# Time mixing in diagonal blocks of 64 tokens, in opposite quadrants of the array

## The reference

```python
def step(state, inp):
    r_t, w_t, k_t, v_t, kk_t, a_t = inp
    sa = jnp.einsum('bhvk,bhk->bhv', state, -kk_t)
    state = (state * w_t[:, :, None, :] + sa[..., None] * (kk_t * a_t)[:, :, None, :]
             + v_t[..., None] * k_t[:, :, None, :])
    return state, jnp.einsum('bhvk,bhk->bhv', state, r_t)
...
_, ys = lax.scan(step, s0, xs)
```

## Time and profile before

| What | Value |
|---|---|
| Time, median of 3 runs | 2509.83 us (2509.53 to 2512.68) |
| Profiled execution | 2512.97 us, its span 2511.3 us |
| PE busy | 2338.5 us (93%), 15533 instructions |
| PE weight loads busy | 1588.8 us (63%) |
| DVE busy | 777.9 us (31%) |
| ACT busy | 365.3 us (15%) |
| Chain that ended last | PE 86%, DVE 11%, ACT 1%, issue 1% |
| Mean granted TensorE clock | 0.937 |

### The profile page before, as it was taken

How to read it: one execution, slowest core, us unless ns; L and a number is a source line. 1 busy time by engine, 2 the same in 40 slices (tenths; PEclk the granted TensorE clock), 3 DMA queues, 4 the chain that set the end, 5 groups by cost and what they waited for, 6 DMA issues and landing times.

```text
span 2511.3 us, 35417 instructions
## 1 busy us (share of the span) xinstructions
PE 2338.5 (93%) x15533; PEld 1588.8 (63%) x15533; DVE 777.9 (31%) x1511; ACT 365.3 (15%) x746; POOL 0.2 (0%) x4
## 2 busy tenths in 40 slices
PE   8887899999987799999999999988889999989998
PEld 5686577766677576655545546455657776656775
DVE  2546346512545420011010010013734652641001
ACT  2411200011421210000000101013220001221001
POOL 0000000000000000000000000000000000000000
PEclk9976899999977799999999999998889999979999
DMA  5210398504210189989989989613229840308410
GB/s 216 84 51 1 119 427 328 193 1 164 94 51 1 71 336 405 394 347 392 410 350 418 425 334 361 262 70 147 107 108 419 323 190 26 109 35 354 154 54 17
DMA packets 55167, 524.08 MB, mean 209 GB/s; under 512 B 6368, under 2 KB 6880, under 8 KB 16864
## 3 DMA queue, kind: packets, MB, share of 16 engines
q1 hardware_dynamic: 45792, 471.43, 46.5%
q10 hardware_dynamic: 9216, 50.34, 5.3%
HBM read 520.69 MB, written 1.05 MB: 208 GB/s over the span
## 4 chain that ended last, share of the span: by engine, by line
PE 86%; DVE 11%; ACT 1%; issue 1%; DMA 0%; DVEq 0%; SPq 0%; ACTq 0%
PE ps L89 86%; DVE ring L89 6%; DVE stat L89 1%; DVE transposed L89 1%; DVE natural L89 1%; DVE gates L89 1%; ACT ring L89 0%; DVE residual L89 0%; DMA ring<-in_moe 0%; ACT z L89 0%; ACT L89 0%; ACT stat L89 0%; DMA constants<-in_const 0%; ACT transposed L89 0%; DVE z L89 0%
## 5 line engine op out<-in xcount | busy, mean ns | idle before, releaser
L89 PE MATMUL ps<-ring 128*32 128x256 f32 (+9 forms) x7636 | 587.5, 345 | 14.9 <-DVE ring L89 5.3
L89 PEld LDWEIGHTS ps<-ring 128*32 128x32 f32 (+4 forms) x7636 | 409.3, 129 | 188.3 <-issue 63.5
L89 PE MATMUL ps<-transposed,ring 128*128 128x256 f32 x2112 | 466.4, 379 | 5.2 <-issue 2.3
L89 PE MATMUL ps<-ring,transposed 128*128 128x384 f32 (+4 forms) x1408 | 470.6, 493 | 0.1
L89 PE MATMUL ps<-ring,z 128*32 128x512 f32 (+2 forms) x1936 | 459.1, 594 | 0.6 <-issue 0.3
L89 PEld LDWEIGHTS ps<-transposed,ring 128*128 128x128 f32 x2112 | 401.0, 190 | 85.8 <-issue 31.2
L89 PEld LDWEIGHTS ps<-ring,transposed 128*128 128x128 f32 x1408 | 266.6, 194 | 188.6 <-issue 65.4
L89 DVE TENSOR_TENSOR z<-z,ps 128x256 f32<-128x256 f32 (+3 forms) x146 | 58.7, 402 | 885.4 <-ACT z L89 855.3
L89 PEld LDWEIGHTS ps<-ring,z 128*32 128x32 f32 (+2 forms) x1936 | 169.4, 139 | 213.1 <-issue 203.7
L89 ACT ACTIVATE z<-ps 128x256 f32<-128x256 f32 (+2 forms) x151 | 56.2, 372 | 943.5 <-PE ps L89 933.6
L89 ACT COPY z<-ps 128x384 f32<-128x384 f32 (+6 forms) x166 | 67.9, 409 | 699.0 <-PE ps L89 697.4
(11 more groups left out here) (129 smaller groups left out, 1147.3 us busy)
## 6 DMA issues: line engine op xcount, KB each, us to landing
ring<-in_moe SPq DMA_DIRECT2D x88, 2048.0 KB, 12.0
ring<-in_ffn SPq DMA_DIRECT2D x66, 1536.0 KB, 15.3
ring<-in_moe SPq DMA_DIRECT2D x88, 1024.0 KB, 10.4
ring<-in_w_in SPq DMA_DIRECT2D x26, 1536.0 KB, 6.8
z<-in_ada ACTq DMA_DIRECT2D x48, 768.0 KB, 6.9
ring<-in_w_out SPq DMA_DIRECT2D x12, 1536.0 KB, 6.3
natural<-in_ada ACTq DMA_DIRECT2D x16, 768.0 KB, 8.1
ring<-in_ple_gate SPq DMA_DIRECT2D x4, 1536.0 KB, 6.5
```

Source lines behind the costliest of these rows:

```text
L89: self.ins = None if self.book.counting else op(*args, **kw)
```

## The change

The parts of the time mixing that stay inside a chunk now compute only the blocks on the diagonal. A masked square is stored as 128 partitions by 64 columns: partitions 0 to 63 hold the block of the first chunk, 64 to 127 that of the second. The masks shrink alike, and `ident64` is a stacked pair of identities. Where one product of 128 by 128 stood, two of 64 by 64 stand, c = 0 from partitions 0 to 63 to PSUM partitions 0 to 63 and c = 1 from 64 to 127 to 64 to 127: opposite quadrants, in the same bank. The functions `rw_inv`, `rw_invT` and `chunk` name these pieces.

All squares of one tile's scores (i) fit into two banks, so both tiles' scores are issued together before the last projection tile and masked by two DVE instructions per tile. The inverse and its transpose lie side by side in `gates`, and an update fills one bank per half, so that one subtraction does both. The first turn is a product with `ident64` instead of a transpose. The copies of the kp factor go ahead, behind the last level. Both layers have the change.

```diff
-    strict, incl = (s < t) & same, (s <= t) & same
-    one["mask4"] = np.concatenate([strict, incl, strict, incl], 1)
+    sc, tc = s % 64, np.arange(64)[None, :]
+    one["ident64"] = (sc == tc)
+    one["mask4"] = np.concatenate([sc < tc, sc <= tc, sc < tc, sc <= tc], 1)
...
-    rw_prod = Carve(work, rw_shared)(8, 4, P)
+
+    rw_prod = Carve(work, rw_shared)(8, 4, HD)
     xc, gc = Carve(xt_flat), Carve(gates_flat)
-    rw_inv, rw_invT, rw_lev, rw_cx = xc(8, P), xc(8, P), gc(8, P), gc(8, P)
-    rw_n, rw_u, rw_yg = rw_inv, rw_lev, rw_cx
+    rw_inverse, rw_lev, rw_cx = gc(2, 2, 4 * HD), gc(8, HD), gc(8, HD)
+    rw_n, rw_u = xc(8, P), xc(8, P)
...
+    def chunk(c):
+        return slice(HD * c, HD * c + HD)
+
+    def rw_inv(c, e):
+        return rw_inverse[chunk(c), e // 4, 0, (e % 4) * HD:(e % 4 + 1) * HD]
...
-    def pe_rw_prod(l, e):
+    def pe_rw_prod(l, i):
 
         pe.part("rw")
-        i, hh = divmod(e, 4)
-        lo_p, b = 64 * (hh % 2), 2 + e % 3
-        pe.wait_ge(f"rw.krT{l}" if e < 3 else f"rw.prod{l}{e - 3}")
-        rhs = rw_pr[lo_p:lo_p + 64, hh // 2, i].rearrange("p a t -> p (a t)")
-        for n, src in enumerate((rw_qT, rw_hT)):
-            mm(ps[:, b, 256 * n:256 * n + 256], src[lo_p:lo_p + 64, hh // 2, i * P:(i + 1) * P], rhs)
-        pe.then_inc(f"rw.score{l}{e}")
+        pe.wait_ge(f"rw.krT{l}", f"ga.out{l}")
+        for pair in range(2):
+            for n, src in enumerate((rw_qT, rw_hT)):
+                for c in range(2):
+                    for par in range(2):
+                        rows, at = chunk(par), i * P + HD * c
+                        mm(ps[chunk(c), 2 + 2 * par + i, (2 * pair + n) * P:(2 * pair + n + 1) * P], src[rows, pair, at:at + HD],
+                           rw_pr[rows, pair, i, :, chunk(c)])
+        pe.then_inc(f"rw.score{l}{i}")
...
     def dve_rw_first(l):
         dve.part("rw")
-        dve.wait_ge(f"mix{l}.proj71", f"ga.out{l}")
         dve_rw_level(l, 0)
...
             pe.wait_ge(f"rw.cx{l}{n}{g}")
-            for e in range(4):
-                mm(ps[:, b, e * P:(e + 1) * P], rw_invT[:, 4 * g + e, :], rw_cx[:, 4 * g + e, :])
-                mm(ps[:, b + 1, e * P:(e + 1) * P], rw_cx[:, 4 * g + e, :], rw_invT[:, 4 * g + e, :])
+            for e in range(4 * g, 4 * g + 4):
+                at = (e % 4) * HD
+                for c in range(2):
+                    mm(ps[chunk(c), 4 + g, at:at + HD], rw_invT(c, e), rw_cx[chunk(c), e, :])
+                for c in range(2):
+                    mm(ps[chunk(c), 4 + g, 256 + at:256 + at + HD], rw_cx[chunk(c), e, :], rw_invT(c, e))
             pe.then_inc(f"rw.xlx{l}{n}{g}")
 
     def dve_rw_inverse(l, n):
         dve.part("rw")
         for g in range(2):
-            b = rw_banks(n)[1 - g]
             dve.wait_ge(f"rw.xlx{l}{n}{g}")
-            for dst, at in ((rw_inv, b), (rw_invT, b + 1)):
-                half = dst[:, 4 * g:4 * g + 4, :]
-                dve(V.tensor_tensor, half, half, bank(at, e=4), ALU.subtract)
-            dve.then_inc(f"rw.inv{l}{n}{g}")
+            both = rw_inverse[:, g].rearrange("p a n -> p (a n)")
+            dve(V.tensor_tensor, both, both, ps[:, 4 + g, :], ALU.subtract).then_inc(f"rw.inv{l}{n}{g}")
+
+    def dve_rw_kp(l):
+
+        dve.part("rw")
+        dve.wait_ge(f"mix{l}.proj71")
+        for i in range(NT):
+            dve(V.tensor_copy, rw_n[:, 4 * i:4 * i + 4, HD:P], rw_kp[:, i, :].rearrange("p (h d) -> p h d", h=4))
...
@@ -2467,13 +2492,11 @@
         pe_rw_turn(l, 3)
         pe_at_turn_k(l)
         win(7, 0)
-        for e in range(3):
-            pe_rw_prod(l, e)
+        for i in range(NT):
+            pe_rw_prod(l, i)
         win(7, 1)
         pe_at_turn_q(l, 0, "rot")
         pe_at_turn_q(l, 1, "rot")
-        for e in range(3, 8):
-            pe_rw_prod(l, e)
         pe_at_turn_pairs(l, 0)
```

More of the change, by code:

```diff
@@ L1049, in act_rw_turn, with dve_rw_prod @@
         act(S.copy, dst, bank(b, a=2, i=NT)).then_inc(f"rw.{name}T{l}")
[L1051 removed]
+    def pe_rw_prod(l, i):
         pe.part("rw")
[L1054 to L1066 removed]
+        pe.wait_ge(f"rw.krT{l}", f"ga.out{l}")
[7 more added lines that the diff above has]
+        pe.then_inc(f"rw.score{l}{i}")
+    def dve_rw_prod(l, i):
+        dve.part("rw")
+        dve.wait_ge(f"rw.score{l}{i}")
+        mask = spread(C("mask4"), 1, 2)
+        for par in range(2):
+            out = rw_prod[:, 4 * i:4 * i + 4].rearrange("p (a b) n t -> p a b (n t)", b=2)[:, :, par]
+            dve(V.tensor_tensor, out, bank(2 + 2 * par + i, a=2), mask, ALU.mult)
+        dve.then_inc(f"rw.prod{l}{i}")
     def dve_rw_level(l, n):
@@ L1076, in dve_rw_first @@
         dve.part("rw")
-        dve.wait_ge(f"mix{l}.proj71", f"ga.out{l}")
         dve_rw_level(l, 0)
-        dve(V.tensor_tensor, rw_invT, spread(C("ident"), 1, 8), rw_lev, ALU.subtract).then_inc(f"rw.first{l}")
+        for g in range(2):
+            dve(V.tensor_tensor, rw_inverse[:, g, 1].rearrange("p (e t) -> p e t", e=4), spread(C("ident64"), 1, 4),
+                rw_lev[:, 4 * g:4 * g + 4, :], ALU.subtract).then_inc(f"rw.first{l}{g}")
     def pe_rw_first(l):
         pe.part("rw")
-        pe.wait_ge(f"rw.first{l}")
         for g in range(2):
-            for e in range(4):
-                turn(2 + g, e * P, rw_invT[:, 4 * g + e, :])
+            pe.wait_ge(f"rw.first{l}{g}")
+            for e in range(4 * g, 4 * g + 4):
+                for c in range(2):
+                    mm(ps[chunk(c), 2 + g, (e % 4) * HD:(e % 4 + 1) * HD], rw_invT(c, e), C("ident64")[chunk(c)])
             pe.then_inc(f"rw.firstturn{l}{g}")
@@ L1092, in act_rw_first @@
             act.wait_ge(f"rw.firstturn{l}{g}")
-            act(S.copy, rw_inv[:, 4 * g:4 * g + 4, :], bank(2 + g, e=4)).then_inc(f"rw.inv{l}0{g}")
-    def rw_banks(n):
-        return (2, 4) if n % 2 else (4, 2)
+            act(S.copy, rw_inverse[:, g, 0], ps[:, 2 + g, 0:4 * HD]).then_inc(f"rw.inv{l}0{g}")
     def pe_rw_lx(l, n):
@@ L1103, in pe_rw_lx @@
         for g in range(2):
-            b = rw_banks(n)[0] + g
             pe.wait_ge(f"rw.inv{l}{n - 1}{g}")
-            for e in range(4):
-                mm(ps[:, b, e * P:(e + 1) * P], rw_lev[:, 4 * g + e, :], rw_inv[:, 4 * g + e, :])
+            for e in range(4 * g, 4 * g + 4):
+                for c in range(2):
+                    mm(ps[chunk(c), 2 + g, (e % 4) * HD:(e % 4 + 1) * HD], rw_lev[chunk(c), e, :], rw_inv(c, e))
             pe.then_inc(f"rw.lx{l}{n}{g}")
@@ L1141, in pe_rw_hv @@
             i, hh = divmod(e, 4)
-            mm(ps[:, 4, e * HD:(e + 1) * HD], rw_prod[:, e, 2, :], rw_v[:, i, hh * HD:(hh + 1) * HD])
+            for c in range(2):
+                mm(ps[chunk(c), 4, e * HD:(e + 1) * HD], rw_prod[chunk(c), e, 2, :], rw_v[chunk(c), i, hh * HD:(hh + 1) * HD])
         pe.then_inc(f"rw.hv{l}")
@@ L1147, in dve_rw_hv @@
         dve.wait_ge(f"rw.hv{l}")
[L1148 to L1151, removed]
+        dve(V.tensor_copy, rw_n[:, :, 0:HD], bank(4, e=8)).then_inc(f"rw.n{l}")
     def pe_rw_solve(l):
@@ L1156, in pe_rw_solve @@
         for g in range(2):
-            for e in range(4):
-                mm(ps[:, 2 + g, e * P:(e + 1) * P], rw_invT[:, 4 * g + e, :], rw_n[:, 4 * g + e, :])
+            for e in range(4 * g, 4 * g + 4):
+                for c in range(2):
+                    mm(ps[chunk(c), 2 + g, (e % 4) * P:(e % 4 + 1) * P], rw_invT(c, e), rw_n[chunk(c), e, :])
             pe.then_inc(f"rw.solved{l}{g}")
@@ L1171, in pe_rw_inside @@
             pe.wait_ge(f"rw.u{l}{g}")
[L1172 to L1176, removed]
+            for e in range(4 * g, 4 * g + 4):
+                at = (e % 4) * P
+                for c in range(2):
+                    m3, u = rw_prod[chunk(c), e, 1, :], rw_u[chunk(c), e, :]
+                    mm(ps[chunk(c), 4 + g, at:at + HD], m3, u[:, 0:HD], True, False)
+                for c in range(2):
+                    mm(ps[chunk(c), 4 + g, at:at + HD], rw_prod[chunk(c), e, 3, :], rw_v[chunk(c), g, (e % 4) * HD:(e % 4 + 1) * HD],
+                       False, True)
+                for c in range(2):
+                    m3, u = rw_prod[chunk(c), e, 1, :], rw_u[chunk(c), e, :]
+                    mm(ps[chunk(c), 4 + g, at + HD:at + P], m3, u[:, HD:P])
             pe.then_inc(f"rw.inside{l}{g}")
@@ L2629, in dve_mixers1 @@
         dve_at_rotate_k(l)
-        for e in range(8):
-            dve_rw_prod(l, e)
+        for i in range(NT):
+            dve_rw_prod(l, i)
         dve_rw_first(l)
```

12 lines of the change are left out of this document (8 added, 4 removed).

## The result

| | before | changed kernel |
|---|---|---|
| Time, median (lowest to highest) of 4 runs each | 2511.26 us (2509.53 to 2516.95) | 2468.69 us (2467.69 to 2470.28) |
| Ratio to before, 95% interval | | 0.9827 (0.981 to 0.9845) |
| Span of the profiled execution | 2511.3 us | 2467.5 us |
| Mean granted clock | 0.937 | 0.943 |
| Mixer of the first layer, from the last decay product's z turns to the turn of the mixed output | 103.94 to 267.26: 163.3 us | 104.34 to 244.81: 140.5 us |

The kernel became 42.6 us faster; 14.4 were forecast. All of it lies where the change is: 22.9 and 21.7 us in the two mixers are 44.6 of the span's 43.8, the rest of the program shifted by less than 1 us. The forecast had 8.0 and 6.4 there.

What follows compares the result with a forecast made beforehand. PE set 86% of the chain and DVE 11%, taking turns in the mixers. Savings of 8.0 and 6.4 us took the profiled 2512.97 to 2498.6; the runs' median lies 3.1 lower, so 2495 us, range 2482 to 2504.

Steps and rivals of the forecast that it cites:

- To 125.47 and to 151.89: First layer's mixer, up to the first inverse round, then through the compression to the next: 3.3 and 5.9 us less.
- Opposite quadrants: Block products in the mixers: a pair of 64-by-64 products runs together, 0.107 us at clock 0.50, about 0.053 at 1.00.
- Which clock: Mixers: PE's clock at 0.50 from the first inverse round to the end, since pairs fill two of four quadrants.
- the pieces to 175.36, 210.28 and 225.82: First layer's mixer, stretches ending at these times, priced at clock 0.50: plus 0.6, minus 1.7 and plus 5.1 us.
- the changes of tile size: Some 14 more places in the first layer where PE's weight load may stand idle, 0.1 us each: plus 1.5.
- The compressed scores: First layer's mixer, stretch 151.89 to 166.50: these products, 2.91 us before, cost 1.0 more at clock 0.50.
- The piece to 186.87: First layer's mixer, from 175.36: subtractions and level shrink, ACT's exponential and weight turns come next; 1.1 us less.
- The clock stays up as now: Rival, both mixers: what ran at clock 1.00 stays so, 14 us less per layer, 2467 us; chance 0.12.
- the last piece: First layer's mixer after 225.82: two turns of scores at clock 0.50, plus 0.8 us; the rest unchanged.
- Opposite quadrants do not run together: Rival, mixers: pairs writing one bank don't overlap, each costs 0.213 us, 32 to 34 more per layer, 2561; chance 0.08.
- the gain is lost in the changes of tile size: Rival, mixers: these changes cost 0.33 us each, 4.6 per layer; total 2503 to 2508 us; chance 0.14.

Runs made afterwards that it cites:

- each level three times: Changed kernel with each of a layer's six level masks computed three times into the same tile; 2487.79 us, ratio 0.9923.
- 30 columns at 97%: Changed kernel with compression products moving 120 columns, plus unread 30-column filling products in four places where PE waits for DVE; 2457.16 us, ratio 0.9782.
- the widened kernel before: Kernel before the change with the compression's 64 matmuls moving 120 columns instead of 30, same result; 2495.90 us, ratio 0.9955.

## Why the prediction was wrong

Its sum can be laid beside two traces: the kernel with one quadrant of each pair, in which the clock was as low as I had assumed, and the changed kernel. Pieces of the first layer, each from one step of the earlier trace rows to the next, the same instruction in each trace; us:

| Piece before | before | forecast | clock low | changed kernel |
|---|---|---|---|---|
| start of the mixer to 125.47 | 21.5 | 18.2 | 18.2 | 18.3 |
| to 151.89 (compression) | 26.4 | 20.5 | 20.9 | 20.9 |
| to 166.50 | 14.6 | 10.6 | 12.0 | 10.3 |
| to 175.36 | 8.9 | 9.5 | 10.3 | 7.9 |
| to 186.87 | 11.5 | 10.4 | 9.3 | 9.4 |
| to 210.28 | 23.4 | 21.7 | 22.2 | 17.0 |
| to 225.82 (solution, inner products) | 15.5 | 20.6 | 21.3 | 14.6 |
| to the end | 41.4 | 42.2 | 42.6 | 42.0 |

*To 125.47 and to 151.89* the forecast holds, by its own steps: DVE free early, then ACT's copies, the blocks' eight instructions and the level; the update halved, one subtraction of 0.70 instead of two. The first rise comes only at the end of the second of these pieces.

*Opposite quadrants* overlap fully: 3.67 us for 32 instructions in one quadrant, 3.68 for 64 in two. The Trainium skill's rule against it ("TensorEngine Tiling (Array Packing)", Restrictions and Gotchas), that different row tiles can't use one PSUM bank at the same time, does not hold for these products, which write both partition halves of one bank.

*Which clock* is the step that failed, in the words "I take 0.50 from the first inverse round to the end of the mixer". I had seen the rises of the earlier trace rows behind whole-array products and concluded that pairs, with half their cells, would not do. The runs show that they do: thinned to one quadrant or to half the columns, the rises go (156.7 us per mixer), with full pairs they are there (140.5), and as filling alone pairs hold the clock much as whole-array products do (0.84 and 0.92 in the late stretch). The conclusion rested on half-array and quadrant products of before at 0.50, and these stand in stretches in which PE also waits: from 230.3 to 267.3 it is busy for 23.79 of 37.00 us. There shape and pauses could not be told apart, and I took the shape alone. The runs show that both count: longer pauses alone kept the clock low (each level three times, 0.50 to 165.4), and so did one quadrant at 95% busy and 30 columns at 97%. One of my readings was also too strict: ahead of the rise at 196.1 us in the kernel before, the update's 128-column products had run for some 2.3 us only, not 3 or more, behind whole-array products of 64 columns. The clock is worth 16.2 us of the first layer's 22.9. In the pieces to 175.36, 210.28 and 225.82 the sum had +0.6, -1.7 and +5.1 at the low clock; they came out as -0.9, -6.4 and -0.9.

*The smaller terms.* With the clock low the sum was 153.7, 155.2 with the changes of tile size, and 156.7 was measured. The compressed scores were mis-sized: 2.91 plus 1.0, measured 4.96. The piece to 186.87 came 1.1 under the forecast. The other pieces together are then some 3 us over their sum, twice the 1.5 I had given the changes of tile size; how much of it these are isn't shown.

*The rivals.* "The clock stays up as now" came nearest: 2467 by its sum, 2468.7 measured, and the clock rose where that rival has it, with dense pairs on both sides of the values. That the totals meet within 2 us is in part luck. The clock didn't stay up everywhere (0.51 from 186.70 to 193.50), the last piece gained nothing where the rival had 0.8, and with the clock low the sum it starts from was itself 3 us short. "Opposite quadrants do not run together" is out by the 3.67 and 3.68 us, "the gain is lost in the changes of tile size" by the total, 34 us under its range.

What the runs don't settle: why the second mixer of the widened kernel before gained 4.2 us and the first 9.7 (the traces show the clock's rises in other places there, no more), and how much of a pause and how small a product the clock bears together.

## What to carry to other kernels

At a stretch of TensorE at the low clock, ask first what its products fill and where it pauses, and only then what they cost. Dense pairs in opposite quadrants raised the clock in these runs, short streams with a full weight load did not. Widening such a stream and filling waits with products nobody reads took off some 30 us more here, the greater part by the widening; at the low clock the change of the algorithm was worth some 12 us for both layers. Issue the two products of a pair next to each other: four of one quadrant and then four of the other cost 34 us here. And where a total moves by less than the sessions differ, go by the stretch that was changed.

## What the hardware showed that I had not expected

- 64 matmuls over 120 columns took 9.34 us in the place where 64 over 30 columns took 13.86.
- The granted clock lay at 0.50 with PE busy 29.18 of 30.00 us. The Trainium skill ("TensorE: Matmul & The Clock Gate", on the clock gate) speaks of how busy PE has been; the trace doesn't agree if that is the profile's busy time.
- The same products in another order cost 34 us more: 5.99 us for an update against 3.68.
- Filling with one quadrant's products kept the clock at 1.00 from 148.20 to 195.90 us and left it at 0.50 from there to 223.2.
